# One-core decoder step: x first, adaptive groups mixed into the first feed-forward block, final norm joined to the last one

## The reference, cut to what matters

```
ada = silu(c) @ w_ada + b_ada               # c: 1 prompt row + 8 sample rows -> 9 x 9216 (shift, scale, gate x 3)
h = rmsnorm(x, g1) * (1 + scale1) + shift1
x = x + 0.5 * gate1 * (silu(h @ Wa) * (h @ Wb)) @ Wo          # FFN 1
x = x + gate2 * mixer(rmsnorm(x, g2) * (1 + scale2) + shift2)   # gated gMLP and mLSTM branches
x = x + 0.5 * gate3 * FFN2(rmsnorm(x, g3) * (1 + scale3) + shift3)
fin = silu(c) @ w_ada_final + b_ada_final    # final shift and scale, 9 x 2048
y = rmsnorm(x, g_final) * (1 + scale) + shift
rmsnorm(x, g) = x * rsqrt(mean(x * x) + 1e-6) * g
```

## Time and profile before

| | us |
|---|---|
| time, median of 3 runs (lowest to highest) | 3016.11 (3016.05 to 3017.38) |
| the profiled execution's own time | 3018.74 |
| its span (first to last instruction) | 3017.03 |
| busy over the span: PE, DVE, ACT, POOL | 2869.1 (95%), 1452.0 (48%), 866.0 (29%), 131.2 (4%) |
| mean granted clock of TensorE, as a share of full speed | 0.974 |
| 0 to 87.1: `bring_in` | 87.1 |
| 150.81: block 0 of FFN 1 starts its down products | |
| 2180.5 to 2981: FFN 2; its last block starts at 2906.47 | 800 |
| 2981 to 3017.03: `final_norm` | 36 |

### The profile page before, as it was taken

How to read it: one execution, slowest core, us unless ns; L and a number is a source line. 1 busy time by engine, 2 the same in 40 slices (tenths; PEclk the granted TensorE clock), 3 DMA queues, 4 the chain that set the end, 5 groups by cost and what they waited for, 6 DMA issues and landing times. The chain is left out here.

```text
span 3017.0 us, 44375 instructions
## 1 busy us (share of the span) xinstructions
PE 2869.1 (95%) x17489; PEld 2753.6 (91%) x17489; DVE 1452.0 (48%) x3014; ACT 866.0 (29%) x1396; POOL 131.2 (4%) x190
## 2 busy tenths in 40 slices
PE   5899999999998999999999999999899999999997
PEld 4799999999998999889988988998799999999996
DVE  4655545445435644336345433634674433344346
ACT  5422222222213412332333233233431111111114
POOL 2100000000003010000000000000200000000002
PEclk7999999999999999999999999999999999999998
DMA  6123222232211122212111221211111111111111
GB/s 229 51 90 98 97 95 86 97 97 83 70 43 29 43 80 72 74 32 68 50 56 32 65 74 32 68 50 56 47 45 42 56 42 42 42 42 42 42 42 60
DMA packets 167523, 192.98 MB, mean 64 GB/s; under 512 B 7760, under 2 KB 157036, under 8 KB 167349
## 3 DMA queue, kind: packets, MB, share of 16 engines
q1 hardware_dynamic: 166962, 191.12, 19.9%
q10 hardware_dynamic: 342, 0.15, 0.0%
q0 software_dynamic: 96, 0.00, 0.0%
HBM read 172.38 MB, written 18.87 MB: 63 GB/s over the span
## 5 line engine op out<-in xcount | busy, mean ns | idle before, releaser
L521 DVE SCALAR_TENSOR_TENSOR xT<-ps,gate_p,xT 128x384 f32<-128x384 f32 (+1 forms) x624 | 348.2, 571 | 115.5 <-PE ps L801 97.5
L907 PE MATMUL ps<-hhi,mw_hi 128*128 128x384 f32 (+1 forms) x1152 | 393.9, 342 | 9.5 <-DVE mw_lo L1684 7.4
L908 PE MATMUL ps<-hlo,mw_hi 128*128 128x384 f32 (+1 forms) x1152 | 380.8, 331 | 0.0
L909 PE MATMUL ps<-hhi,mw_lo 128*128 128x384 f32 (+1 forms) x1152 | 380.3, 330 | 0.0
L738 DVE TENSOR_TENSOR hf<-st,ps 128x384 f32<-128x384 f32 x132 | 70.2, 532 | 642.4 <-PE ps L822 640.4
L820 PE MATMUL ps<-hhi,wa_hi 128*128 128x384 f32 (+1 forms) x1056 | 350.0, 331 | 16.5 <-DVE wa_lo L728 13.6
L821 PE MATMUL ps<-hlo,wa_hi 128*128 128x384 f32 (+1 forms) x1056 | 347.6, 329 | 0.0
L822 PE MATMUL ps<-hhi,wa_lo 128*128 128x384 f32 (+1 forms) x1056 | 347.2, 329 | 0.0
L820 PE MATMUL ps<-hhi,wb_hi 128*128 128x384 f32 (+1 forms) x1056 | 346.2, 328 | 0.3 <-DVE wb_lo L728 0.3
L822 PE MATMUL ps<-hhi,wb_lo 128*128 128x384 f32 (+1 forms) x1056 | 346.0, 328 | 0.0
L821 PE MATMUL ps<-hlo,wb_hi 128*128 128x384 f32 (+1 forms) x1056 | 345.9, 328 | 0.0
(11 more groups left out here) (295 smaller groups left out, 5166.7 us busy)
## 6 DMA issues: line engine op xcount, KB each, us to landing
ada_raw<-in_w_ada SPq DMA_DIRECT2D x36, 1024.0 KB, 5.1
mw_raw<-in_w_in SPq DMA_DIRECT2D x32, 1024.0 KB, 5.9
wa_raw<-in_w_ffn_in SPq DMA_DIRECT2D x22, 1024.0 KB, 5.1
wb_raw<-in_w_ffn_in SPq DMA_DIRECT2D x22, 1024.0 KB, 5.2
wo_raw<-in_w_ffn_out SPq DMA_DIRECT2D x22, 1024.0 KB, 5.0
ada_raw<-in_w_ada_final SPq DMA_DIRECT2D x8, 1024.0 KB, 5.3
cs<-in_state_mlstm_C SPq DMA_DIRECT2D x32, 256.0 KB, 2.8
out_C_sample<-cs SPq DMA_DIRECT2D x32, 256.0 KB, 2.2
```

The lines of the kernel that those rows point to most:

```text
L521: ins = dve.scalar_tensor_tensor(out=xT[:, m, t0:t0 + wp], in0=ps[:, bank, 0:wp], scalar=gate_p[:, m:m + 1], in1=xT[:, m, t0:t0 + wp], op0 ...
L907: pe.matmul(out, wh, xh, start=(j == 0), stop=False)
L908: pe.matmul(out, wh, xl, start=False, stop=False)
L909: ins = pe.matmul(out, wl, xh, start=False, stop=(j == last))
```

## The change

**Front.** `bring_in` is no longer a block with a barrier: it becomes an object whose parts the engines of FFN 1 run ahead of their own (`lead`). The sums of squares are made from x before it is turned: ACT squares a token tile and sums it along the row in one instruction (`accum_out`), POOL makes the mean and raises it to -0.5 (128 x 9 values), DVE makes nine diagonal matrices of that, and nine float32 matmuls with the constant matrix spread them over the partitions as `rr`. That takes the place of the squares on `xT`, POOL's adds, the means, roots and reciprocals of FFN 1. Eight adaptive groups stay in the lead, in the order 0, 4, 1, 5, 2, 6, 3, 7, so that every second one completes a pair of feature tiles; the first three are native float32 products, the other five are split as before. Each has its own raw buffer, and the loads of the first up weights stand behind the fifth. PE's order then mixes them with the products of unit 0 of block 0, two feature tiles at a time (`lead_pair`: 2 tiles x a, b x 2 halves x 3 matmuls), and four more groups with the rest of block 0. The other 32 groups stay in blocks 1 to 8.

**Back.** `final_norm` has no block of its own. In FFN 2's lead, POOL spreads the final shift along rows (`columns`), PE turns it by 16 matmuls (`shift_rows`), ACT copies it out in four pieces (`keep_shift_rows`). The last block's down units come in another order (`final.order`: units 0 and 2 by pairs of m, then unit 1 for all m) on four PSUM banks instead of six. ACT makes z = xT * factor behind each square, PE sums the squares of a token tile into a column (`sums`), ACT and DVE take root and reciprocal of 128 x 6 and 128 x 3 values, PE turns z (`turn`, 4 transposes for half a tile) between the last down units, and DVE multiplies and adds the shift row in one instruction on its way to the store (`keep`).

The core of the diff (of the front, then of the back):

```diff
-        def bring_in():
+        def bring_in(norm):
+            ORDER = [0, 4, 1, 5, 2, 6, 3, 7]
+                def load(self, sp, load_up):
...
+                    for j, g in enumerate(ORDER):
+                        if j == 5:
+                            load_up("a", 0)
+                            load_up("b", 0)
+                        sp.dma_start(first_raw[j][:, :, :], wa_d[:, :, g * 256:g * 256 + 256]).then_inc(first_in[j].sem, 16)
...
+                    def square(tt):
...
+                        act.activation(junk[rows, tt % 2, :], xtok[rows, tt, :], ACT.Square, accum_out=sums[rows, tt:tt + 1]).then_inc(squared.sem, 1)
...
+                    pool.wait_ge(squared.sem, NTT)
+                    pool.tensor_scalar(var[:, :], sums[:, :], 1.0 / D, EPS, ALU.mult, ALU.add).then_inc(made.sem, 1)
+                    pool.wait_ge(*made(7))
+                    pool.tensor_tensor(rr_t[:, :], var[:, :], power[:, :], ALU.pow).then_inc(made.sem, 1)
...
+                    self.product(pe, 0)
...
+                        ins = pe.matmul(ps[:, t // 3, 128 * (t % 3):128 * (t % 3) + rows], mean[0:rows, :], diag[0:rows, t, 0:rows],
+                                        start=True, stop=True)
...
+                    for j in range(1, 5):
+                        self.product(pe, j)
+                        self.turn(pe, j - 1)
+                    up_pair(0)
+                    self.turn(pe, 4)
+                    self.product(pe, 5)
+                    up_pair(1)
+                    self.turn(pe, 5)
+                    self.product(pe, 6)
+                    self.product(pe, 7)
+                    self.turn(pe, 6)
+                    up_pair(2)
+                    self.turn(pe, 7)
+                    up_pair(3)
...
+                    def lead_up():
+                        ada_product(pe, group(0, 0))
+                        for i, n in FIRST_ORDER[2:]:
+                            q = FIRST_ORDER.index((i, n)) - 2
+                            up("a", i, n, 0)
+                            up("b", i, n, 0)
+                            ada_turn(pe, group(0, q))
+                            if q < 3:
+                                ada_product(pe, group(0, q + 1))
...
+                order = [(2 * p + i, n) for p in range(KT // 2) for n in (0, 2) for i in range(2)] + [(m, 1) for m in range(KT)]
...
+                    pool.tensor_copy(col[:, :, :], ada[:, ADA_T:ADA_T + KT, 0:1].broadcast_to([P, KT, P])).then_inc(col_made.sem, 1)
+                    for i in range(2):
+                        pool.tensor_copy(col_s[:, :, i, :, :], bc(ada[:, ADA_T:ADA_T + KT, 1:9], 3, STOK)).then_inc(col_made.sem, 1)
...
+                        act.activation(dst[:, 512 * (b % 2):512 * (b % 2) + 512], ps[:, 4 + b, :], ACT.Copy).then_inc(shift_kept.sem, 1)
...
+                    pe.wait_ge(*squares_added((14, 21)[part]))
...
+                    dve.scalar_tensor_tensor(out=dst, in0=ps[r, bank(i), :], scalar=rr_t[r, c:c + 1],
+                                             in1=(shift_s if t == 8 else shift)[r, f], op0=ALU.mult, op1=ALU.add
+                                             ).then_inc(kept.sem, 1)
...
+                            if final and last and u >= 19:
+                                final.keep(dve, 2 * (u - 19))
+                                final.keep(dve, 2 * (u - 19) + 1)
...
+                                if u == 17:
+                                    final.sums(pe, 0)
+                                for i in range(2 * (u - 18), 2 * (u - 17)) if u >= 18 else ():
+                                    final.turn(pe, i, out_added)
...
-        ffn(I["w_ffn2_in"][0], I["w_ffn2_out"][0], Norm(V_FFN2, 48, 56, gate=64, factor=0.5))
-        final_norm(Norm(V_FINAL, ADA_T, ADA_T + KT, final=True))
+        ffn(I["w_ffn2_in"][0], I["w_ffn2_out"][0], Norm(V_FFN2, 48, 56, gate=64, factor=0.5),
+            final=final_norm(Norm(V_FINAL, ADA_T, ADA_T + KT)))
```

More of the change, by code:

```diff
@@ L669, in body @@
                     def body(b, ada_too, last):
+                        if lead and first(b):
+                            lead_body()
+                            return
                         if ada_too:
@@ L718, in _ @@
                 def _(pool):
+                    if lead:
+                        lead.gpsimd(pool)
+                    if final:
+                        final.columns(pool)
                     for u in range(24):
@@ L780, in body @@
                                 split(*{9: ("a", 0), 13: ("b", 0), 17: ("a", 1)}[u], b + 1)
[L782 to L790 removed]
+                        if final and last:
+                            for i in range(10, 12):
+                                final.keep(dve, i)
+                            final.inverses(dve, 1)
+                            for i in range(12, 18):
+                                final.keep(dve, i)
+                    if lead:
+                        lead.vector(dve, split)
+                    else:
+                        norm.factors(dve)
+                        norm.unit(dve, 0, between=lambda: split("a", 0, 0))
+                        split("b", 0, 0)
+                        split("a", 1, 0)
+                        split("b", 1, 0)
+                        norm.unit(dve, 1)
+                        norm.unit(dve, 2)
+                        norm.samples(dve)
+                        norm.gates(dve)
+                    if final:
+                        final.factors(dve)
                     blocks(dve, body, own)
@@ L839, in body @@
                         pe.wait_ge(*C["o_lo"](b * 2 + 2))
-                        for u, (m, n) in enumerate(OUT_ORDER):
+                        banks = 4 if final and last else 6
+                        for u, (m, n) in enumerate(final.order if final and last else OUT_ORDER):
                             t0, w = UNITS[n]
@@ L854, in body @@
                             ins.then_inc(C["out_unit"].sem, 1)
-                            if ada_too and u == 2:
+                            if ada_too and u == 2 and not first(b):
                                 ada_turn(pe, group(b, 3))
-                    norm.means(pe)
+                            if final and last:
+                                if u == 17:
+                                    final.sums(pe, 0)
+                                for i in range(2 * (u - 18), 2 * (u - 17)) if u >= 18 else ():
+                                    final.turn(pe, i, out_added)
+                        if final and last:
+                            for i in range(12, 14):
+                                final.turn(pe, i, out_added)
+                            final.sums(pe, 1)
+                            for i in range(14, 18):
+                                final.turn(pe, i, out_added)
+                    if lead:
+                        lead.tensor(pe, lead_pair)
+                    else:
+                        norm.means(pe)
+                    if final:
+                        final.shift_rows(pe)
                     blocks(pe, body)
```

886 lines of the change are left out of this document (574 added, 312 removed).

## The result

The changed kernel takes 2982.3 us (median of four runs, 2981.08 to 2983.4) against 3016.49 (3016.05 to 3017.38) beside it: 0.9886 of the time before, 95% interval 0.9869 to 0.9903. The profiled execution took 2982.70, with a span of 2980.7.

| stretch | before | after | change | predicted |
|---|---|---|---|---|
| start to the first up product | 99.34 | 47.07 | -52.27 | -52.0 |
| start to block 0's first down unit | 150.81 | 128.74 | -22.07 | -22.6 |
| rest of FFN 1 | 815.44 | 815.55 | +0.11 | 0 |
| mixer | 1214.39 | 1216.24 | +1.85 | 0 |
| FFN 2, release of the barrier to the first up product | 10.11 | 12.52 | +2.41 | +4.9 |

A forecast was written before the change was run, and what follows sets the result against it. PE was taken as the bound, idling in the first 99.3 us, at FFN 2's start and behind the last down unit. 3018.74 - 22.6 + 4.9 - 20.1 = 2980.9, less 2.63 to the median, plus 0.7: 2979, range 2968 to 2997.

The forecast's parts named there:

- The front: Start to block 0's first down unit: 128.2 us instead of 150.81, a gain of 22.6, likely 15 to 27.
- the first pair: First two feature tiles of up products in the lead: start at 47.3, stop at the b half until wb is split by 59.
- Its reason: Front: mixing fills PE's waits, with 16.7 us of up products done inside group time by 77.
- The walk: Front: queues of PE, ACT, DVE, POOL and SP followed in the new order with measured durations, giving 128.2.
- Rival B: Front: bound by ACT, DVE and low clock, pairs only trade places with groups; gain 8 to 13, 2989 to 2996; chance 0.11.
- FFN 2's lead: Start of FFN 2: first up product 15.1 after the release instead of 10.2, a loss of 4.9 us (1.5 to 8.5).
- The end: Last block's first down unit to the end: 43.1 us instead of 63.2, a gain of 20.1 (16 to 22.5).
- wait and sums: End, behind 18 down units: PE waits 2.0 us for the sum of POOL's 14 adds.
- Rival C: End slowed by POOL's adds beside DVE, and FFN 2's lead by POOL's copies at 7.9: 2988; chance 0.06.
- The sum: Whole kernel: 3018.74 - 22.6 + 4.9 - 20.1 = 2980.9, as a median 2978.3, with 0.7 for small waits 2979.
- Rival D: Front: clock stays low through block 0's up products, first down unit at about 165; 3023 in all; chance 0.03.
- E: Whole change: an early wait and the wait for the sums undo it; 3008 to 3020; chance 0.04.

The follow-up runs named there:

- e_unmixed: The changed kernel with the lead's last four split groups first on PE and the four pairs of up products behind them; 2976.99 us (0.9863).
- ctl: The changed kernel run again unchanged, as the measure for other runs on the same chip; 2979.11 us (0.9883).
- e_best1: The changed kernel with block 0's groups split earlier, shift copies singly behind tiles 4, 5, 9, 10, and sums after the nineteenth down unit; 2969.64 us (0.9844).
- e_sums: The changed kernel with the squares of the first six token tiles summed after the nineteenth down unit instead of the eighteenth; 2979.01 us (0.9867).
- e_unmixed2: PE's order of e_unmixed, with the single late shift copies and the later sums of e_best1; 2968.36 us (0.9834, on another chip).
- e_copies: The changed kernel with ACT's shift-row copies moved behind the rounding of tiles 8 and 16; 2982.82 us (0.9888).

## Why the prediction was right, and where not

**The front** came out at 128.74 for 128.2, and so did its marks: `rr` spread from 26.73 (26.8), the first pair at 47.07 (47.3), the last pair done at 81.35 - 2.73 = 78.6 (77), the rest of block 0 in 50.1 (51). One row it got wrong without harm: the first pair was said to stop at its b half until 59 and stopped for 0.86, since ACT and DVE split wb next. A native group is 3.62, inside its bounds of 2.9 and 5.8.

**Its reason failed in part.** "By then PE has done 16.7 us of up products inside what was group time" is true of the trace, but it is not where the time went: without any mixing N to D is 99.0 in two runs, with it 104.7 to 106.3 in five. The walk priced this one order and none beside it. What is left as the cause can be read from the marks of e_unmixed and of the kernel before, whose first group starts at 37.04:

```profile
21.49 2.36 DVE L234 TENSOR_TENSOR ada_lo<-ada_raw,ada_hi 128x1024 fp32r<-128x1024 f32 x2 [7.43 <-ACT ada_hi L227]
```

```profile
37.04 0.40 PE L242 MATMUL ps<-ada_hi,cs_r 128*18 128x256 f32 x1 [3.46 <-DVE cs_r L363]
```

The first group starts at 26.13 instead, 10.9 earlier: before, the copies of `xT` that PE waited 7.56 for stood on DVE behind the low half of the first group, which itself waited 7.43 for ACT's rounding; now the first groups are native and need no half. Eight groups and the spreading of `rr` then take 42.5 us (26.13 to 68.65), twelve groups took 50.1: 7.5, though a group now takes longer. And the norm's chain of 12.2 is gone. Together that is the 30.7 from 99.34 to 68.65. Block 0 from there to its first down unit takes 56.50 instead of 51.47, because four groups are in it: a net of 25.7. That is an account of rows; none of the three was put back by itself. Rival B's mechanism, pairs that trade places with groups at a low clock, was at work (0.84 in ctl's window), but with 5.7 to 7.2 us and not the 10 to 15 it was given.

The Trainium skill ("TensorE: Matmul & The Clock Gate", HAM oscillation) warns that a clock falls back when work stops for waits again and again. The trace agrees: 0.84 and 0.91 mixed, and unmixed 0.70 among the groups and 1.00 behind them. The clock alone does not decide, since the unmixed order has the lower one first and still ends earlier; DVE's halves, which come earlier, are the other part, and how the 5.7 us divide between the two isn't shown.

**FFN 2's lead** was mis-sized: +2.41 for +4.9, inside its bounds. POOL's copies took 2.26 and not 4.0, so the matmuls began at 2163.30, 2.8 after the release, and the rounding at 7.8 instead of 10.3. The 64 x 1024 add of two operands was the wrong neighbour for a copy, and the memset (0.95 for 1024 columns; the copy took 1.03) the right one. The 1.8 cycles a column of the Trainium skill ("GPSIMD Engine Reference", Elementwise — side-by-side cycle accounting), from which 3.1 was estimated, are too dear here as well: 2.26 for 2048 columns; the measurement decides.

**The end** was mis-sized by 1.2: 18.9 for 20.1. By terms, measured (predicted): 18 units 17.7 (17.8); wait and sums 3.2 (2.0), a term in which the sums themselves stood at nothing, and six one-column products take 1.71; six units 12.9 (11.7), the first of them 3.3 at half clock and then five of 1.92 (1.95); last chain 3.4 (2.9); six `keep` 4.04 (4.1); from there to the end 3.1 (4.65). Rival C did not come: L690 took 0.51 beside POOL's adds, L531 had taken 0.53.

**The sum** therefore came as near as it did partly by luck: two misses offset each other (the lead cost 2.5 less than said, the end gained 1.2 less), and the mixer's +1.85 is chance. Of the 3.3 us between 2979 and 2982.3, 1.5 come from the step to the median: the profiled execution lay 2.63 above it before and 0.4 after, and 0.7 had been added. Rival D is excluded by a clock of 0.93 up to 128.7, E by every mark.

## What to carry to other kernels

When a starved engine is given other work to fill a wait, look at what that work is put ahead of: pairs of products ahead of short turns that DVE waits for made PE wait later, while one pair just behind such a turn gained 3.4 to 4.5 us over none at all. Price the plain order beside the clever one, since the same walk does both. A copy out of PSUM that must happen sometime belongs on its engine where the work in front of it is already there and the next has slack: the same four copies cost 2.4 ahead of the rounding, 4.8 behind tiles 8 and 16, and nothing singly behind tiles 4, 5, 9 and 10. And before an engine is called short, look whether it idles: in e_best1 DVE was late and had stood still for 5.57 us.

## What was not expected of the hardware

- ACT's square with a sum along the row takes a second instruction: 1071 ns for 128 x 1024 and 212 more for reading the sum.

```profile
L463 ACT ACTIVATE squares<-xtok 128x1024 f32<-128x1024 f32 x8 | 8.5, 1071 | 2.4 <-DMA xtok<-in_x_prompt 2.4
L463 ACT ACTIVATION_READ_ACCUMULATOR squares<-xtok 128x1 f32 x8 | 1.7, 212 | 0.0
```

- A float32 product of a single column takes 1.50 / 6 = 0.25 us in e_sums and 1.71 / 6 = 0.28 in the changed kernel, as much as one of 128 columns (2.38 / 9 = 0.26).
- The turns of x, the same 72 in every version, end at 22.4 in ctl and at 26.1 in e_unmixed, because the clock differs: 1.00 there and 0.57 here from 14.5 to 22.4. Ahead of that PE had waited 2.38 for the small vectors' DMA in e_unmixed. The row behind that wait, and the window:

```profile
15.02 0.99 PE L635 MATMUL ps<-ident,crow 9*128 9x9 f32 x8 [2.38 <-DMA vrow<-in_gmlp_ln_g]
```

```profile
14.50:22.40 7.90, 7.38 (x39) 7.03 (x39) 3.50 (x7) 3.93 (x11) 0.00 (x0) 0.57 1.08 307
```

That the longer wait brought the clock down is not shown (1.35 and N at 24.0 in e_unmixed2, 1.37 and 23.3 in e_copies). Loading those vectors earlier was not tried.
